# Input projections, first block: products of tokens that lack the norm's factor, which VectorE multiplies in on the way out of PSUM

## The reference, cut to what matters here

```python
def rmsnorm(x, g):
    xf = x.astype(F32)
    y = xf * lax.rsqrt(jnp.mean(xf * xf, axis=-1, keepdims=True) + EPS)
    return (y * g.astype(F32)).astype(x.dtype)

hn = rmsnorm(h, mix_norm[l])                      # h: 2048 tokens x 1024
a_q, a_f, a_i, a_g, b_y, b_x, c_u, d_z = jnp.split(hn @ w_in[l], IN_SPLITS, axis=-1)
```

## Time and profile before

| | us |
|---|---|
| median of 3 runs | 3208.75 |
| lowest and highest | 3208.48, 3211.06 |
| the profiled execution, device time | 3205.94 |
| its span in the profile | 3204.2 |
| TensorE busy in it | 3034.6 (95%) |
| first matmul of product 0 starts | 15.91 |

### The profile page before, as it was taken

One profiled execution on the slowest core, in us unless ns is written; L12 is line 12 of the kernel. 1 busy time (PEld: TensorE's weight loads), 2 busy tenths in 40 slices (PEclk: granted clock), 3 DMA queues, 4 the chain that ended last, 5 costly groups with the idle time before them and its releaser, 6 DMA issues. The chain is left out here.

```text
span 3204.2 us, 51255 instructions
## 1 busy us (share of the span) xinstructions
PE 3034.6 (95%) x20608; PEld 2500.1 (78%) x20608; DVE 2169.0 (68%) x3314; ACT 1332.6 (42%) x2125; POOL 498.5 (16%) x650
## 2 busy tenths in 40 slices
PE   8999997899989799989999899999899999999998
PEld 6777776788888578758888678888688887888887
DVE  6777676777647577454454587777877777787786
ACT  5657656555541422123333343333433333444443
POOL 4344343757620011000000000000000000000000
PEclk9999998999999899999999999999899999999999
DMA  6566555221200544321211323323333334876873
GB/s 214 150 192 188 166 176 157 68 70 62 82 20 18 179 172 154 108 92 42 70 61 64 132 92 112 119 106 138 105 112 119 108 117 131 275 215 215 254 219 123
DMA packets 200072, 416.20 MB, mean 130 GB/s; under 512 B 15280, under 2 KB 99504, under 8 KB 193456
## 3 DMA queue, kind: packets, MB, share of 16 engines
q1 hardware_dynamic: 199856, 413.18, 39.3%
HBM read 295.66 MB, written 117.46 MB: 129 GB/s over the span
## 5 line engine op out<-in xcount | busy, mean ns | idle before, releaser
L2999 PE MATMUL ffn_ps<-ffn_t_p,ffn_w_p 128*128 128x512 f32 x2640 | 606.1, 389 | 2.6 <-DVE ffn_w_p L3172 2.6
L2999 PEld LDWEIGHTS ffn_ps<-ffn_t_p,ffn_w_p 128*128 128x128 f32 x2640 | 495.2, 188 | 106.4 <-DVE ffn_w_p L3172 3.6
L3014 PE MATMUL ffn_ps<-ffn_t_p_parts 128*128 128x512 f32 x1416 | 329.3, 392 | 5.7 <-DVE ffn_t_p_parts L3314 5.7
L3014 PEld LDWEIGHTS ffn_ps<-ffn_t_p_parts 128*128 128x128 f32 x1416 | 267.8, 189 | 62.5 <-DVE ffn_t_p_parts L3314 6.6
L420 POOL TENSOR_TENSOR w_low<-w_ring,w_high 128x1024 fp32r<-128x1024 f32 x84 | 215.2, 2565 | 313.1 <-ACT w_high L574 313.1
L3025 ACT ACTIVATE ffn_w_p<-ffn_w_p_sums 128x512 fp32r<-128x512 f32 x132 | 83.4, 632 | 339.4 <-DVE ffn_w_p_sums L3193 339.1
L536 PE MATMUL proj<-hn_high,w_high 128*128 128x512 f32 x544 | 222.0, 416 | 2.2 <-ACT hn_high L564 1.6
L536 PE MATMUL proj<-hn_high,w_low 128*128 128x512 f32 x544 | 209.4, 394 | 0.0
L536 PE MATMUL proj<-hn_low,w_high 128*128 128x512 f32 x544 | 207.5, 390 | 0.0
L3014 PE MATMUL ffn_ps<-ffn_t_p 128*128 128x512 f32 x696 | 162.5, 389 | 0.0
L3095 ACT ACTIVATE ffn_t_p_parts<-ffn_ring 128x1536 fp32r<-128x1536 f32 x59 | 87.7, 1487 | 157.7 <-PE ffn_ps L3014 154.2
(11 more groups left out here) (519 smaller groups left out, 6661.0 us busy)
## 6 DMA issues: line engine op xcount, KB each, us to landing
ffn_ring<-in_w_up SPq DMA_DIRECT2D x44, 1024.0 KB, 5.3
ffn_ring<-in_w_down SPq DMA_DIRECT2D x88, 512.0 KB, 5.5
w_ring<-in_w_feat SPq DMA_DIRECT2D x84, 512.0 KB, 4.0
ffn_ring<-scratch_values SPq DMA_DIRECT2D x88, 257.0 KB, 4.6
scratch_gates<-ffn_gate SPq DMA_DIRECT2D x44, 512.0 KB, 2.6
ffn_ring<-scratch_gates SPq DMA_DIRECT2D x88, 256.0 KB, 3.7
scan_in<-scratch_scan SPq DMA_DIRECT2D x16, 896.0 KB, 4.4
scratch_values<-ffn_raw SPq DMA_DIRECT2D x22, 513.0 KB, 3.5
```

What stands on the lines that cost most here:

```text
L2999: mm = pe.matmul(bank(name, s), w_part(name, a)[:, k * P:(k + 1) * P], t_part(name, b)[:, k * TB:(k + 1) * TB], start=k == a == b == 0, st ...
L3014: mm = pe.matmul(ps[:, DOWN_BANKS[2 * t + c]], down_part(n, x)[:, HID + t * TC:HID + (t + 1) * TC], down_part(n, y)[:, c * DH:(c + 1) * DH ...
```

## The change

For block 0 alone, the tokens are multiplied by the gain but not by the factor. Their high part is made by ACT with the gain as scale, the low part by DVE in one instruction with the gain. The loads go out as `prm`, w0, turned tiles, w1, `cst`, the four tiles of x, the rest, w2. The factor's spreading moves on TensorE from ahead of product 0 to behind product 2. VectorE copies the spread factor to SBUF once (`first_wide`) and takes all 17 products of block 0 out of PSUM itself, multiplying by it (`take_first`); ACT then only applies the function in place where there is one (`IN_PLACE`: four tiles), and still converts the slices in the same places. The four token tiles at the block's end are taken by ACT as before, with the factor as scale. Blocks 1 to 3 are unchanged. The diff, cut to its core:

```diff
+    def load_gains(sp):
+        sp.dma_start(prm[:], D["prm"]).then_inc(C["first_loaded"], 16)
+
     def load_first(sp):
-        for dst, src in ((cst[:], D["cst"]), (prm[:], D["prm"])):
-            sp.dma_start(dst, src).then_inc(C["first_loaded"], 16)
+        sp.dma_start(cst[:], D["cst"]).then_inc(C["cst_loaded"], 16)
...
+        first_wide = tok[:, CB - 1]
...
-            for j in range(CB):
-                load_x(0, j)
-            C["load_first"](sp)
+            C["load_gains"](sp)
             load_w(0)
             load_x_turned(0)
             load_w(1)
+            C["load_first"](sp)
+            for j in range(CB):
+                load_x(0, j)
             C["load_rest"](sp)
             load_w(2)
...
-            pe.wait_ge(C["first_loaded"], C["first_loaded_n"])
...
-                if p:
+                if p == 0:
+                    pe.wait_ge(C["cst_loaded"], C["cst_loaded_n"])
+                else:
                     pe.wait_ge(*x_normed.at(p - 1))
...
                     small_products(n)
+                    if n == 2 and p == 0:
+                        spread_rstd(0)
...
-            spread_rstd(0)
             blocks(run)
...
             def high_tokens(p):
                 for k in range(KT):
-                    act.wait_ge(*x_normed.at(p, k))
                     if p:
+                        act.wait_ge(*x_normed.at(p, k))
                         act.wait_ge(*free_at(p, k))
-                    act.activation(hn[0][:, k], x_turned[:, k], ACT.Copy).then_inc(hn_high.sem, 1)
+                        act.activation(hn[0][:, k], x_turned[:, k], ACT.Copy).then_inc(hn_high.sem, 1)
+                    else:
+                        act.wait_ge(*xt_in[k].at(0))
+                        act.activation(hn[0][:, k], x_turned[:, k], ACT.Copy, scale=col("mix_norm", k)).then_inc(hn_high.sem, 1)
...
                 def take(n, dst, func=ACT.Copy):
-                    act.wait_ge(*proj_done.at(p, n))
-                    own.done(act.activation(dst, proj[:, n % 3], func), proj_out, n)
+                    if p:
+                        act.wait_ge(*proj_done.at(p, n))
+                        own.done(act.activation(dst, proj[:, n % 3], func), proj_out, n)
+                    else:
+                        act.wait_ge(*proj_out.at(0, n))
+                        if n in IN_PLACE:
+                            own.done(act.activation(dst, dst, func), first_func, IN_PLACE.index(n))
                     high_behind(n)
...
+            act.wait_ge(C["first_loaded"], C["first_loaded_n"])
+            high(0, 0)
+            high_tokens(0)
+            high(0, 1)
             for j in range(CB):
                 squares(0, j)
             norm_root(0)
-            high(0, 0)
-            high_tokens(0)
-            for n in range(1, WR):
-                high(0, n)
+            high(0, 2)
             blocks(run)
...
+            def first_low_tokens():
+
+                for k in range(KT):
+                    dve.wait_ge(*hn_high.at(0, k))
+                    dve.scalar_tensor_tensor(hn[1][:, k], x_turned[:, k], col("mix_norm", k), hn[0][:, k], ALU.mult, ALU.subtract)\
+                       .then_inc(hn_ready.sem, 1)
+
+            def first_factors():
+
+                own = Own(dve, first_own)
+                own.done(dve.tensor_copy(first_rstd[:], rstd[:]))
+                dve.wait_ge(*wide_ready.at(0))
+                own.done(dve.tensor_copy(first_wide, rstd_wide[:]))
+                dve.sem_inc(x_normed.sem, KT)
...
+                def take_first(n, dst):
+
+                    if p == 0:
+                        dve.wait_ge(*proj_done.at(0, n))
+                        own.done(dve.tensor_tensor(dst, proj[:, n % 3], first_wide, ALU.mult), proj_out, n)
+
                 for n in range(Z_TILES):
                     if n == 3:
                         dve.wait_ge(*r_stored.at(p, back=1))
+                    take_first(n, z[:, n, 1:])
                     dve.wait_ge(*proj_out.at(p, n))
...
+            first_low_tokens()
             mean_square(0)
+            dve.wait_ge(C["cst_loaded"], C["cst_loaded_n"])
             diagonals(0)
-            normed(0)
-            low_tokens(0)
+            first_factors()
             blocks(run)
```

More of the change, by code:

```diff
@@ L40 @@
 Z_TILES = 7
+IN_PLACE = (9, 10, 13, 14)
 SCAN = ("q", "k", "cum", "r", "kp", "kk", "b", "csig")
@@ L100, in load_constants @@
          "lora": lora, "lru_w": lru_w, "loaded": sem("constants_loaded"), "loaded_n": 3 * 16,
-         "first_loaded": sem("constants_first"), "first_loaded_n": 2 * 16,
+         "first_loaded": sem("constants_first"), "first_loaded_n": 16, "cst_loaded": sem("constants_cst"), "cst_loaded_n": 16,
          "prepared": sem("constants_prepared")}
@@ L148, in prepare_on_dve @@
         dve.memset(d[7], 0.0).then_inc(C["prepared"], 1)
+    C["load_gains"] = load_gains
     C["load_first"], C["load_rest"], C["prepare_on_act"], C["prepare_on_dve"] = load_first, load_rest, prepare_on_act, prepare_on_dve
@@ L213, in project_and_prepare @@
         rstd = sb("rstd", [P, CB])
+        first_rstd = sb("first_rstd", [P, CB])
         z = sb("z", [P, Z_TILES, 1 + TB])
@@ L254, in project_and_prepare @@
         k_ready = sig("k_ready")
+        first_func = sig("first_func", 2 * G2)
         out_b, out_b_sq, b_root = sig("out_b"), sig("out_b_sq"), sig("b_root")
@@ L260, in project_and_prepare @@
         dve_own, act_own = sig("s1_dve_own").sem, sig("s1_act_own").sem
-        norm_dve = sig("norm_dve_own").sem
+        norm_dve, first_own = sig("norm_dve_own").sem, sig("first_own").sem
         s1_hold = sig("s1_hold").sem
@@ L695, in run @@
                     act.wait_ge(*tok_done.at(p, j))
-                    own.done(act.activation(tok[:, j], tok_bank[j], ACT.Copy), tok_out, j)
+                    own.done(act.activation(tok[:, j], tok_bank[j], ACT.Copy, scale=1.0 if p else first_rstd[:, j:j + 1]), tok_out, j)
                 if has_next:
@@ L769, in convolve @@
                                                           ALU.mult, ALU.add))
+                take_first(7, bx[:, 0, LRU_TAPS - 1:])
                 convolve(0)
@@ L776, in run @@
                              vaux_out, t)
+                take_first(8, bx[:, 1, LRU_TAPS - 1:])
                 convolve(1)
@@ L788, in run @@
                     own.done(dve.tensor_scalar(T["inv"][:, t], aux_v[:], 1e-24, None, ALU.max), vaux_out, 2 + t)
+                    take_first(9 + t, T["by"][:, t])
                 for t in range(G2):
@@ L800, in run @@
                                                       ALU.mult, ALU.mult), rk_ready, t)
+                    take_first(11 + t, T["f"][:, t])
                 if has_next:
@@ L806, in run @@
                              *((f_clamped,) if t else ()))
+                take_first(13, T["q"][:, 0])
                 for t in range(G2):
@@ L809, in run @@
                     own.done(dve.tensor_tensor(T["bonus"][:, t], z[:, 5 + t, 1:], aux_v[:], ALU.mult), vaux_out, 4 + t)
+                    take_first(*((15, T["ag"][:, 0]) if t else (14, T["q"][:, 1])))
                 if has_next:
                     normed(p + 1)
+                take_first(16, T["ag"][:, 1])
                 dve.wait_ge(*f_log.at(p))
```

## The result

The changed kernel takes 3217.26 us (median of 9 runs, 3213.98 to 3222.06) against 3208.75 before (median of 9, 3207.69 to 3214.29); the ratio is 1.0026, 95% interval 1.0017 to 1.0034. The forecast was 3213.0, with a range up to 3217.0: the way it went was right, the size was half of it, and the time lies 0.3 us above the range.

What follows compares the result with a forecast made beforehand. TensorE, busy 95% of the span, was taken as the bound. 6.6 us gained at the start, minus 6.4 chain, minus 4.4 clock, is -4.2, so 4.2 slower: 3213.0 us, range 3208 to 3217.

Steps and rivals of the forecast that it cites:

- product 2's start: Block 0's front: TensorE starts product 2 at 25.9 instead of 32.48, leaving 6.6 us of head start.
- Nothing there returns time, and a shift passes to the end one for one: Work after the front: later slack covers the delays, so the start's shift reaches the end unchanged.
- a wait at the change to block 1: Sign of being wrong: TensorE waits again where block 0 gives way to block 1.
- the head start can't be kept: Front of block 0: 6.6 us gained at product 2 are lost again; product 3 starts at 39.4, 1.5 later.
- w2's landing: Initial loads: w2 still lands behind the same 7200 KB, at 22.3, and product 2 needs it.
- the chain I had at 6.4 us: Before product 3: spreading, copy, take of product 0, w3's conversion and POOL's subtraction; 6.4 us, 5.3 of it idle.
- product 0: Program's front: waits for `w_low(0)` and starts at 8.3 instead of 15.91.
- The clock: Restarts after TensorE's two stops: 1.7 us lost in product 2 and 2.7 in product 3, 4.4 together.
- rival B: VectorE becomes the bound and product 12 comes 4.4 us later: +8.3, 3217; chance 0.10.
- A (little clock loss): TensorE's clock doesn't fall at the first stop, 1.7 us lost at the second: +1.5, 3210.3; chance 0.22.
- C (w3 not late): Product 3 starts right behind the spreading, the head start stays: -5.5 at most, 3203.3; chance 0.04.
- D: Each of TensorE's two stops costs the same, 1.7 us: 3212.0; chance 0.12.

Runs made afterwards that it cites:

- e3: The kernel before with 15 further matmuls on TensorE behind product 2 of the first block, to end the first stage 3.4 us late: 3212.9 us.
- e5: The changed kernel with 22 further matmuls between the factor's spreading and product 3, filling TensorE's second stop: 3213.8 us.
- e6: The changed kernel with 22 further matmuls before product 3 and 12 between products 1 and 2, to fill both stops: 3213.0 us.
- e7: The changed kernel, but in block 0 ScalarE converts slice n + 3 first and waits for VectorE's take only afterwards: 3213.4 us.
- e4: The changed kernel with the factor's spreading behind product 1 instead of product 2: 3206.9 us.
- e8: The changed kernel with the spreading behind product 1, w2 loaded right behind w1 and converted before the squares: 3205.8 us.

## Why the prediction was right or wrong

**The step that failed is the size of the sum, at two terms; its mechanism held.** The first is product 2's start, 25.9 in the sum and 26.98 in the mean of the four profiles: 1.1 us. The second is the sentence "Nothing there returns time, and a shift passes to the end one for one": from product 8 to the end of the stage 0.9 to 1.0 us more were lost, which the sum had at nothing (a wait at the change to block 1 was among the prediction's own signs of being wrong). The range, in turn, left out how far executions of one kernel lie apart.

**Right: that the head start can't be kept.** The three pieces of the argument are in the profile. w2's landing sets product 2 (ScalarE idle until 23.09 for the DMA), the slice w3 then hangs behind the spread factor, and the chain I had at 6.4 us took 6.39 in all four profiles of the changed kernel, with 5.34 idle where I had 5.3.

**Product 2's start was put 0.7 to 1.4 us too early** (25.9; it is 26.62 to 27.27). I scaled the old landing of w2, 22.3, by bytes; in the new order it lands at 23.1 or later. One difference is that w3's load, before issued 4 us behind w2, now follows it at once; that this is the cause wasn't tried. At product 0 (8.3 forecast, 10.12) I had missed ScalarE's table load: before, it stood at the program's very start (0.88), and now it begins only when w0 has landed (5.24 + 1.28). (The row names `hn_high`, but GpSimd's first subtraction ended at 10.02, 0.1 before product 0.) Product 1 then started at 18.00 and not at 16.9, so TensorE idled 3.02 us before product 2, not 3.5. Here this cost nothing at the end, because product 2 waits for w2 anyway.

**The clock was right in the mean and wrong as a fixed sum.** I had 1.7 and 2.7, 4.4 together. The four profiles gave 0.1 + 1.9, 2.8 + 2.3, 1.6 + 1.8 and 2.9 + 2.5: 2.0 to 5.4, mean 4.0. The two stops cost 1.9 and 2.1 on average, nearly alike, where I had the longer one 1.0 dearer; its upper bound of 3.4 stands in no row, and the most that it cost was 2.5. The single rows from which I priced it were samples of something that changes with each execution.

**Losses further on in the stage were put at nothing** and are 0.9 to 1.0 us from product 8 to the end of the stage. The rows:

```profile
80.03 1.06 ACT L587 ACTIVATE w_high<-w_ring 128x1024 fp32r<-128x1024 f32 x1 [7.00 <-DVE bx L786]
...
83.28 1.48 ACT L662 ACTIVATE t_sq<-z,prm_sb 128x512 f32<-128x512 f32 x2
...
84.06 1.12 PE L486 MATMUL aux_v<-t_sq,cst 128*128 128x512 f32 x2
...
155.75 2.44 PE L545 MATMUL proj<-hn_low,w_high 128*128 128x512 f32 x8
```

ScalarE's `take(8)` now waits 7.00 us for VectorE, so its squares of k (L662) are 0.4 us late for TensorE's L486; I had looked for late slices and late banks only, and not at the work that ScalarE has behind the takes. At the turn to block 1 a pass over the low parts of the tokens takes 2.44 us instead of 1.98; VectorE makes these parts from 152.72 to 157.63, while the pass, begun at 155.75, already runs.

**The sum, corrected.** The forecast's +4.2, plus 1.1 (product 2), minus 0.4 (clock, mean), plus 0.9 (late losses), is 5.8, the mean of the table's four profiles at 557 us. The kernel before had -0.3 there in its mean, so 6.1 separate the first stages. The means of the times are 7.4 apart, with a standard error of 0.7, and the 5.8, a mean of four values from 3.5 to 7.5, has one of 0.9. So the 1.3 between aren't clear of noise and stay open; e3, e5, e6 and e7 show no such surplus, e4 and e8 one of 1.5 and 0.4. What is left to 3217.3 is the base: 3208.75 for the kernel before was 1.2 under its mean of 3209.9.

**The range failed at one step:** its upper edge was built from the terms of the first stage (+3 to +6.5) and from half of rival B. It had no term for what the later stages add by themselves, though the kernel before alone runs from 3204 to 3216. A median of three runs was taken as if it were exact. Nor do its terms add up to +3 to +6.5: chain 6.2 to 6.9, clock 3.4 to 5.3 and w2 by half a us, less the 6.6 gained, are +2.5 to +6.1; nothing hangs on it, as the upper edge of 3217 is that of rival B.

**The rivals.** A (little clock loss) was the case in one of four profiles, the first. B (VectorE the bound) didn't occur: in the rest of the block nothing but the 0.4 us named is lost. C (w3 not late) needed another place of the spreading; e4 is what it looks like. D, by the Trainium skill's "TensorE: Matmul & The Clock Gate", section "HAM oscillation — how this bites in real kernels", has each gap make the next burst start cold, at the same price. Here gaps of 3.24 us and more did, at 1.6 to 3.0 us, and e5's of 2.71 us too, at 1.8; the changed kernel's of 3.02 us did not. So the length of the stop alone doesn't decide. On average both stops cost much the same, as D had it, at 4.0 together, between D's 3.4 and my 4.4.

## What to carry to other kernels

When work is moved off the front of a program, ask which later step waits for it, and in which engine's queue the next weights stand behind that wait; here a step of 1 us was put where nobody could hide it, and half of what it cost in turn was TensorE's clock after the stop. A barrier belongs in a stop that exists already (e4), and a load that ends a stop should be issued ahead of loads that aren't waited for as soon (e8: 1.1 us more in the first stage of its profile). And before a range is given for one per mille of a kernel, look how far its own executions lie apart: the profiled one may be a lucky one.

## What the runs showed of the hardware

- TensorE's granted clock after nearly the same idle time isn't the same in each execution: after 2.71 us idle (e5) 1.8 us were lost, after 3.02 us none, after 3.24 us 2.8, after 3.88 us 1.6, after 4.16 us 2.9 and after 4.20 us (e7) 3.0.
- In the scan over chunks, which has stops of its own, the same kernel loses 0 or about 3.5 us at the same place (granted clock 0.99 or 0.50 from 659 to 666 us). With it two executions of one kernel differ by over 7 us, all of it behind the first 550.
- VectorE takes a 128x512 product out of PSUM with a multiplication by an SBUF tile in 0.69 us, also while GpSimd subtracts (L786 at 62.52 in the changed kernel, inside GpSimd's 59.89 to 67.58), where VectorE's step with two operands in SBUF (L796) takes 2.90 us beside GpSimd at 36.09 and 0.76 without it at 55.47.
- One VectorE instruction on 128x256 in SBUF that began within a train of GpSimd instructions took 8.86 us in two of fourteen profiles (e6 at 568.48, e7 at 568.51) and 0.5 to 1.0 in the others, at the same place of the program.
